# Moving the stores of the gate blocks from SyncE's DMA queue to ScalarE's in a hybrid decoder layer

## The reference, cut to what matters

```python
z = rmsnorm(x, g_mix) @ w_in            # the gate columns mo, ga, gb: 20 blocks of 128
...
logits = einsum('bthd,bshd->bhts', qb, k) * F_SCALE + f_cum[t] - f_cum[s]   # masked, per head
p = softmax(logits); y = einsum('bhts,bshd->bthd', p, v)
...
x + (sigmoid(ga) * a + sigmoid(gb) * b) @ w_out
```

## Time and profile before

| | |
|---|---|
| median of 3 runs | 2133.38 us |
| lowest and highest | 2132.53 and 2136.48 us |
| the profiled execution | 2136.39 us |
| its span, first to last instruction | 2134.7 us |
| mean granted TensorE clock | 0.954 of 2.4 GHz |
| PE busy over the span | 1936.5 us, 91% |
| phase 3, heads 0 to 7 | 468.81 to 859.39 us of the span |

### The profile page before, as it was taken

How to read it: one execution, slowest core, us unless ns; L and a number is a source line. 1 busy time by engine, 2 the same in 40 slices (tenths; PEclk the granted TensorE clock), 3 DMA queues, 4 the chain that set the end, 5 groups by cost and what they waited for, 6 DMA issues and landing times.

```text
span 2134.7 us, 31432 instructions
## 1 busy us (share of the span) xinstructions
PE 1936.5 (91%) x12117; PEld 1811.3 (85%) x12117; DVE 818.2 (38%) x1486; ACT 542.5 (25%) x930; POOL 642.6 (30%) x473
## 2 busy tenths in 40 slices
PE   2999999979998989465979899999999999999898
PEld 2777788868998989444979899999999999998798
DVE  4500233226655655422563232233323332235333
ACT  5311234224444543112322211001100011003311
POOL 0414223032222222002225634334333434335121
PEclk8999999989999999777999899999999999999899
DMA  4222543153323231565321211111111111120111
GB/s 126 70 87 83 172 158 117 67 156 98 95 76 99 76 95 41 181 237 209 106 90 49 69 40 39 43 55 49 49 39 39 59 39 39 41 83 25 36 56 41
DMA packets 203277, 177.78 MB, mean 83 GB/s; under 512 B 49046, under 2 KB 168058, under 8 KB 203162
## 3 DMA queue, kind: packets, MB, share of 16 engines
q1 hardware_dynamic: 156890, 159.92, 23.6%
q10 hardware_dynamic: 45280, 16.58, 3.2%
q0 software_dynamic: 1024, 0.13, 0.1%
HBM read 139.52 MB, written 39.24 MB: 84 GB/s over the span
## 4 chain that ended last, share of the span: by engine, by line
PE 81%; DVE 7%; issue 3%; ACT 3%; DMA 2%; SPq 2%; POOL 1%; ACTq 0%; DVEq 0%; POOLq 0%
PE pair L2396 26%; PE bank L2396 21%; PE bank L2089 7%; PE bank L2220 7%; PE bank L2066 5%; PE pair L2204 3%; PE pair L2066 2%; PE pair L2188 1%; PE pair L2286 1%; DMA scratch_yT<-yb 1%; DVE yb L1737 1%; PE pair L2177 1%; PE pair L2166 1%; SPq L796 1%; PE pair L2050 1%
## 5 line engine op out<-in xcount | busy, mean ns | idle before, releaser
L2396 PE MATMUL bank<-acth,wha 128*128 128x352 f32 x640 | 212.4, 332 | 31.6 <-DVE actl L1889 16.8
L2396 PE MATMUL bank<-actl,wha 128*128 128x352 f32 x640 | 209.6, 328 | 0.0
L2396 PE MATMUL bank<-acth,wla 128*128 128x352 f32 x640 | 209.1, 327 | 0.0
L2220 PE MATMUL bank<-acth,fwh 128*128 128x352 f32 x480 | 162.0, 337 | 15.5 <-POOL fwl L988 15.5
L2396 PE MATMUL pair<-hh,whb 128*128 128x352 f32 x528 | 171.1, 324 | 0.2 <-DVE XR L1994 0.2
L2396 PE MATMUL pair<-hl,whb 128*128 128x352 f32 x528 | 169.2, 320 | 0.0
L2396 PE MATMUL pair<-hh,wlb 128*128 128x352 f32 x528 | 169.0, 320 | 0.0
L1994 DVE TENSOR_TENSOR XR<-XR,pair 128x352 f32<-128x352 f32 x264 | 135.1, 518 | 86.0 <-PE pair L2396 84.8
L1070 POOL TENSOR_TENSOR hl<-un,hh 128x352 fp32r<-128x352 f32 x66 | 62.3, 944 | 342.6 <-ACT hh L1486 342.6
L2220 PE MATMUL bank<-acth,fwl 128*128 128x352 f32 x480 | 155.6, 324 | 0.0
L2220 PE MATMUL bank<-actl,fwh 128*128 128x352 f32 x480 | 155.1, 323 | 0.0
(11 more groups left out here) (442 smaller groups left out, 4803.5 us busy)
## 6 DMA issues: line engine op xcount, KB each, us to landing
raw<-in_w_gu SPq DMA_DIRECT2D x44, 512.0 KB, 3.8
wraw<-in_w_in SPq DMA_DIRECT2D x24, 512.0 KB, 5.8
scratch_zA<-stage SPq DMA_DIRECT2D x48, 256.0 KB, 2.0
raw<-in_w_down SPq DMA_DIRECT2D x22, 512.0 KB, 3.6
scratch_zT<-fout SPq DMA_DIRECT2D x20, 528.0 KB, 3.1
fraw<-in_w_in SPq DMA_DIRECT2D x20, 512.0 KB, 4.9
gs<-scratch_zT SPq DMA_DIRECT2D x16, 528.0 KB, 3.5
kpg<-in_cache_k SPq DMA_DIRECT2D x32, 256.0 KB, 5.2
```

The costliest lines, as they stand in the source:

```text
L2220: ins = nc.tensor.matmul(BANK[u % 2][:, 0:TW], w[:, c % 2, k, :], x[:, k, t * TW:(t + 1) * TW], start=n == 0, stop=n == 3 * KC - 1)
L2396: ins = nc.tensor.matmul(out, w[i](k), x[j](k), start=n == 0, stop=n == total - 1)
```

## The change

SP no longer waits for a gate block's copies and no longer stores it. ACT issues that store itself, right behind the cast of block c + 2 that follows the block's third copy, after a wait on its own semaphore that the copy has ended. SP's loads of the gate blocks stay in their place in SP's list, without the wait that stood before them; what they still wait for is `f_lo`, which says that the buffer of `fraw` has been split.

```diff
-            def store_gate(c):
-                sp.wait_ge(f_out, 3 * c + 3)
-                sp.dma_start(o["zT"][c * P:(c + 1) * P, :], fout[:, c % 2, :]).then_inc(f_st[c % 2], 16)
-
             def store_y(g):
                 sp.wait_ge(y_done, 2 * g + 2 + 2)
...
                     if u % 3 == 2:
-                        store_gate(u // 3)
                         if u // 3 + 3 < NGATE // 3:
                             load_gate(u // 3 + 3)
...
                 nc.scalar.copy(fout[:, c % 2, t * TW:(t + 1) * TW], BANK[u % 2][:, 0:TW]).then_inc(f_out, 1)
-                if t == 2 and c + 2 < NGATE // 3:
-                    gate_high(c + 2)
+                if t == 2:
+                    if c + 2 < NGATE // 3:
+                        gate_high(c + 2)
+                    act.wait_ge(f_out, u + 1)
+                    act.dma_start(o["zT"][c * P:(c + 1) * P, :], fout[:, c % 2, :]).then_inc(f_st[c % 2], 16)
```

## The result

The changed kernel took 2120.89 us in the median of 5 runs (2118.35 to 2123.84), the one before 2133.78 on the same chip: a ratio of 0.994, with a 95% interval of 0.9925 to 0.9954. That is 12.8 us or 0.6% faster. The forecast was 17.0. 2120.89 lies inside the stated range of 2112.5 to 2122, but outside the forecast's own, 2113 to 2120.

What follows compares the result with a forecast made beforehand. PE, busy 91% of the span, was taken as the bound, so gains come only where it stands still: 17.7 gained less 0.7 for stores on ACT is 17.0 us, median 2133.4 to 2116.4, range 2112.5 to 2122.

Steps and rivals of the forecast that it cites:

- What is late, and why: Heads 3 and 6: SP's `yb` store stands behind a wait for ACT, issued 8.0 us late; some 19 us lost.
- The size of that gain: Phase 3 without the stall: heads 3, 6 and 1 save 8.4 + 8.1 + 1.2 = 17.7 us, at most 21.6.
- The clock: PE after the stall in heads 3 and 6: granted clock 0.94 over those heads should become 1.00.
- The stores on ACT: Twenty waits and issues on ACT, mostly hidden behind casts: 0.35 us each in heads 3 and 6, 0.7 in all.
- The gate loads: SP's loads of blocks 3 to 19 go earlier, may stretch ACT's issue of v: taken 0, at worst 8.3 us.
- Crowding: Rival: gate loads, q, k, v and gate store meet in one window, losing 11.1 of 17.7 us: 2126.8; chance 0.08.
- half-way case: Crowding of loads and stores in one window at half its full size: 2121.5 us.
- Only issue time: Rival: `yb` store stays late, only the gate store's issue on SP is saved, 1.0 us: 2132.4; chance 0.04.
- ACT as the bound: Rival: new stores hold ACT ahead of exponentials or casts, 39.6 us lost, 21.9 net: 2155; chance 0.02.
- the larger gain: Rival: all heads of phase 3 become like head 2: 2111.8 us; chance 0.08.
- The signs: `yb` store within 0.5 us of its data, heads 3 and 6 at 46 to 47.1, gate stores 0.3 to 0.5 us.

Runs made afterwards that it cites:

- first experiment: Kernel before, with only SP's store of `yb` moved to position 3, ahead of that position's gate store; nothing moved to ACT: 2117.13 us, ratio 0.9907.
- third experiment: Changed kernel with ACT's gate stores, SP's old wait kept ahead of the gate loads, and the `yb` store ahead of that wait: 2116.68 us, ratio 0.9909.
- fifth experiment: Changed kernel, gate loads still early, with ACT issuing the next head's q, k, v after the split of row block 2: 2118.53 us, ratio 0.9919.

## Why the prediction was right, and where it was not

- **What is late, and why.** Right. The first two experiments show it from both sides: moving the `yb` store alone gives the gain, moving the gate stores alone gives none.
- **The size of that gain.** The forecast had 8.4 for head 3, 8.1 for head 6 and 1.2 for head 1, 17.7 in all. With nothing else changed (first experiment) they measured 55.47 - 46.96 = 8.51, 55.14 - 46.95 = 8.19 and 47.70 - 46.20 = 1.50, and head 4 gave 0.27. Head 0 was the right guide: heads 3 and 6 stopped at 47.0, not at head 2's 45.8.
- **The clock.** Right: all heads are at 1.00, the 2.4 GHz level.
- **The stores on ACT.** Forecast 0.7, from 0 to 1.4 each in heads 3 and 6, with 39.6 in the rival; measured nothing, since head 3 is equal to 0.01 us with and without them (third experiment against the first). The neighbourhood of `load_next`, for which 0.35 each was taken, lengthened none beyond 0.41.
- **The gate loads.** This is the term that was mis-sized: "so I take 0 and keep 8.3 for the range". The stretch itself came as its worst case had it: the seven issues of v took 15.7 us in the changed kernel against 7.1 before, 8.6 more where 8.3 was the bound. How much of it lies on the path was wrong: not 0 but, in the profiled heads, 18.5 - 15.2 = 3.3 us. The reason given was that an issue of 1.98 had cost head 5 nothing. That was true and did not carry on. The change made it 3.08 in head 5, and that cost 46.64 - 45.80 = 0.84. A slack that had held one long issue was taken to hold any. The size is not known well: the ratios of the first and the fifth experiment against the change's would make it 0.33% and 0.21%, some 7 and 4.5 us, with wide intervals.
- **The rivals.** Crowding was named with the right place and given 0.08. In the heads it took 3.3 us, about a third of its worst case of 11.1, and all of it from the loads; the measured time is nearer to its half-way case, 2121.5, than to the forecast's 2116.4. Only issue time, ACT as the bound and the larger gain did not occur.
- **The signs.** The store of `yb`, the waits and the stores on ACT came as they were to come if the prediction was right. Heads 3 and 6, with 48.59 and 47.57, lie above the 46 to 47.1 that were named.
- **What luck there was.** The gain was 0.8 larger than forecast and the stores 0.7 cheaper, and these made up for part of the 3.3: in the heads the sum missed by 1.8 us only.

One difference stays open: the profiled executions lie 16.2 us apart and the medians 12.9. The profiled execution of the kernel before is 2.6 us above its median, that of the changed one 0.7 below; where in the program these differences lie was not measured. The changed kernel's runs spread over 5.5 us, the first experiment's over 5.1, so the spread doesn't come from the long issues alone.

## What to carry to other kernels

A store that somebody waits for must not stand in a queue behind an instruction that waits for somebody else; look at what each queue's waits hold back, and reorder the list first: here one moved line gave more than moving twenty stores to another engine. Taking a wait out of a queue also sets free what stood behind it; ask what that will now run into. The issue of a transfer takes time in the list of the engine that issues it, and here that time grew when the other queue had a load in flight. Put it where that engine idles or, as with the gate stores here, beside a cast that is still running.

## What the runs showed of the hardware

A transfer issued from ACT took longer to issue when SP had 512 KB in flight: v, the third of three loads, took 0.61 to 0.93 us in the median in the four kernels whose gate loads stay late and whose `load_next` stays in its place, and 2.05 to 2.23 in the four in which, in most heads, such a load goes out just ahead of it. Rows of 4 KB did the same as rows of 512 B (2.05 and 2.08). ACT's own gate stores, issued alone, took 0.34 to 0.41 us in the six kernels that have them. Which unit holds the issue back was not tried.

A load of SP's is not the only thing that goes with a long issue. In the same four kernels with late loads the issue of k in head 3 took 1.56 to 1.82 us and that of v in head 5 1.52 to 2.04, and no transfer of SP's was in flight. During each of these the trace shows one transfer of 0.02 MB on the queue that it calls "q8 instruction", and in the kernel before none during the issues of the other five heads. Whether it is the cause was not tried.
